# Memory values in four raw tiles of 256 columns, half of them worked off between the units of the memory attention

## The chip, the cores and the metric

One core of a Trainium2 chip runs the whole kernel. The metric is the device time of one execution in microseconds (us). The engines are TensorE (PE in the profile; its weight loads stand apart as PEld), VectorE (DVE), ScalarE (ACT), GpSimd (POOL) and SyncE (SP), whose queue issues the loads of the weights. The granted clock of TensorE has two levels, 2.4 GHz (1.00 in the rows) and 1.2 GHz (0.50).

## The reference

The kernel computes three transformer blocks in a row on 256 tokens of width 1024, in float32. The change lies in the first block, in and around its memory attention (4 heads of 256, 256 memory rows):

```python
def first_block(...):
    h = layer_norm(ALPHA * h + 0.5 * swiglu(h, ffn1_w1, ffn1_w3, ffn1_w2), ln1_g, ln1_b)
    mix = parallel_mixer(h, ...)                      # ends in (...) @ w_o
    h = layer_norm(ALPHA * h + mix, ln2_g, ln2_b)
    h = layer_norm(ALPHA * h + memory_attention(h, mem, mem_w_q, mem_w_kv, mem_w_o), ln3_g, ln3_b)
    ...

def memory_attention(h, mem, w_q, w_kv, w_o):
    q = (h @ w_q).reshape(B, S, 4, 256)
    k, v = split(mem @ w_kv)                          # each (B, M, 4, 256)
    s = einsum('bqhd,bkhd->bhqk', q, k) * 256 ** -0.5
    o = einsum('bhqk,bkhd->bqhd', softmax(s), v)
    return o.reshape(B, S, 1024) @ w_o
```

The keys and the values depend on `mem` alone, so they can be computed at any time before the attention needs them. The queries need the output of the second layer norm (`ln2`).

## The kernel before

**The weight stream.** All weights are packed on the host into slots of 128 x 1024 floats (512 KB). SP loads them in the order of the stages in `plan()` into a ring of 4 (`ring`); a slot's load waits until the slot four places earlier is free (`load`). There are two kinds of slots. A *split* slot is copied by ScalarE into a rounded high half (`wpair`, L477) and VectorE subtracts to get the low half (L480); its place in the ring is free after the subtraction, and TensorE later multiplies with three terms (high x high, high x low, low x high, in fp32r). There are three `wpair` buffers. A *raw* slot (the `False` in `plan()`: the memory keys and values among others) is read by TensorE straight from the ring in plain float32, which the trace shows as two instructions for each matmul; its place is free only when TensorE has gone on (`hold`, `release`).

**Stages.** `tok` stages (`pe_tok`) hold activations stationary and stream weights, in tiles of 512 columns; `feat` stages (`pe_feat`) hold weights stationary and stream 256 activations. A tile has two halves, t = 0 and 1: ScalarE takes the first out of PSUM and VectorE the second (`lin`). `lin_done0/1` count finished halves, `lin_out0/1` halves that were taken out, and `wait_lin(pe, g)` makes TensorE wait until g tiles have left. Every engine runs its list strictly in the order in which it is written.

**The order around the change**, on TensorE (L1694 to L1706): `memv0` (4 raw slots), with the transposes of `mix` after its 1st and 2nd slot; `wo` (8 split slots); `memv1` (4 raw slots), with the transposes of the normalised rows (`pe_norm`, in four quarters, each as soon as VectorE has written it) after its 2nd slot; `memq` (8 split slots, two tiles); `pe_attn(pe, MEM)`, four units of two heads and 128 queries each; the transposes of its output `mo`; `memo` (8 split slots); `pe_norm("ln3")`.

**The attention** is a pipeline: in step i TensorE computes the scores of unit i, the transposes of the probabilities of unit i-1 and the product with the values of unit i-2. VectorE takes the row maximum of the scores, ScalarE the exponentials and the copy of the transposed probabilities, and VectorE scales the result. `piece(i)` is a place behind the scores of unit i where other work can be put; the first block's other two attentions use it for the gate's weights (`pe_tok_piece`), the memory attention does not.

**Splitting ahead.** `split.begin(name, n)` makes ScalarE or VectorE split the first n slots of a stage at that place of its list; `split.cover(name, n)` splits up to two slots past tile n, but not past the next raw slot (`RUN_END`). Before `memv0` and `memv1` end, the lists read

```python
            act_x(act, "mix")            # and dve_x on VectorE
            split.begin("wo", 2)
            values_out(0)
            split.cover("wo")
            act_sqrt(act, "ln2")
            act_x(act, "ln2")
            split.begin("memq", 2)
            values_out(1)
            lin("memq", 0, ...)
            act_attn(act, MEM)
            act_x(act, "memo")
```

where `act_x` and `dve_x` (L722, L727) bring transposed rows as high and low half into `xpair`. As `memo` follows `memq` with no raw slot between, its first two slots are split while `memq` runs.

Of the kernel before, what the change touches and what calls it, by code (L numbers as in the profile page):

```python
# [30 lines left out]
P = 128  # L31
D = 1024
SEQ = 256
NT = SEQ // P
KD = D // P
# [39 lines left out]
def plan():  # L75

    stages = {}
    slot = tile = 0

    def add(name, kind, cols, ends, split, **more):  # L80
        nonlocal slot, tile
        stages[name] = Stage(kind, slot, tile, cols, ends, split, **more)
        slot, tile = slot + len(cols), tile + len(ends)

    def tok(name, nk, widths, split=True):
        s = Stage("tok", 0, 0, [], [], split, nk=nk)
        cols, ends = [], []
        for w in widths:
            kper = s.per_slot(w)
            cols += [min(kper, nk - k) * w for k in range(0, nk, kper)]  # L90
            ends.append(len(cols))
        add(name, "tok", cols, ends, split, widths=tuple(widths), nk=nk)

    def rows(name, nk, split=False):

        add(name, "rows", [SLOT] * nk, [nk, nk], split)

    def feat(name, ntile, split=True):
        add(name, "feat", [SLOT] * 4 * ntile, [4 * (n + 1) for n in range(ntile)], split)

    def ffn(name):
        add(name, "ffn", [SLOT] * 3 * NF, [3 * NF, 3 * NF], True)

    ffn("ffn0")
    feat("memk0", 1, False)
    tok("proj", KD, (384, 288, 512))
    feat("qkd", 2)
    tok("qb", Q_RANK // P, (384, 384), False)
    tok("kvb", KV_RANK // P, (512, 512), False)
    tok("gate", KD, (512,) * 4)  # L110
    feat("memk1", 1, False)
    tok("upm", 4, (512, 512))
    tok("upd", 4, (512, 512))
    tok("memv0", KD, (512,), False)
    tok("wo", KD, (512, 512))
    tok("memv1", KD, (512,), False)
    feat("memq", 2)
    tok("memo", KD, (512, 512))
    ffn("ffn1")
    for l in range(2):  # L120
        ffn(f"ffn{2 + 2 * l}")
        feat(f"cina{l}", 2)
        tok(f"bin{l}", KD, (512,))
        feat(f"cinb{l}", 2)
        rows(f"wout{l}", KD)
        ffn(f"ffn{3 + 2 * l}")
    tok("qkv", KD, (512,) * 6)
    tok("gatt", KD, (512, 512))
    tok("z", KD, (512,) * 4)
    tok("atto", KD, (512, 512), False)  # L130
    tok("dt", KD, (SSD_H,))
    feat("xbc", 8)
    tok("gssd", KD, (512, 512))
    rows("ssdo", INNER // P, True)
    tok("wo3", KD, (512, 512))
    feat("pq", 4)
    add("peer", "peer", [SLOT] * 2 * NKEY, [2 * NKEY] * 2, True)
    cols, order, run_end, count = [], [], [], [0, 0]
    for st in stages.values():
        for c in st.cols:  # L140
            cols.append(c)
            order.append((st.split, count[st.split]))
            count[st.split] += 1

    run_end = [0] * slot
    end = slot
    for i in reversed(range(slot)):
        if not order[i][0]:
            end = i
        run_end[i] = end  # L150
    return stages, slot, cols, order, run_end
# [64 lines left out]
def pack_stream(x):  # L216
# [3 lines left out]
    def put_tok(name, w):  # L220
        s = STAGES[name]
        slot, c0 = s.slot, 0
        for wd in s.widths:
            kper = s.per_slot(wd)
            blk = w[:, c0:c0 + wd].reshape(s.nk, P, wd)
            for k0 in range(0, s.nk, kper):
                kk = min(kper, s.nk - k0)
                out[slot, :, :kk * wd] = blk[k0:k0 + kk].transpose(1, 0, 2).reshape(P, kk * wd)
                slot += 1
            c0 += wd  # L230
# [27 lines left out]
    put_tok("wo", x["w_o"][0])  # L258
    for j in range(2):
        put_feat(f"memk{j}", x["mem_w_kv"][0][:, j * HALF:(j + 1) * HALF])  # L260
        put_tok(f"memv{j}", x["mem_w_kv"][0][:, D + j * HALF:D + (j + 1) * HALF])
    put_feat("memq", x["mem_w_q"][0])
    put_tok("memo", x["mem_w_o"][0])
    for l in range(2):
# [120 lines left out]
def build(nc, wstream, rows, mixrow, cols, diag, consts, relb, keys, x_tok, xT_in, memT_in, ws, out, tbuf):  # L385
    ctx = ExitStack()
    with ctx:
# [52 lines left out]
        def wait_lin(eng, g):  # L440

            if g > 0:
                for t in range(NT):
                    eng.wait_ge(S(f"lin_out{t}"), g)
# [74 lines left out]
        def bank(g, t):  # L519

            return psum[:, 2 * (g % 2) + t, :]
# [54 lines left out]
        FT0["peer"] = 6 * NF  # L576


        def pe_tok(pe, name, src, ns=range(8), between=lambda i: None):

            s = STAGES[name]
            slot = ([s.slot] + s.ends)[ns[0]]
            for n, w in enumerate(s.widths):
                if n not in ns:
                    continue
                g = s.tile + n
                kper = s.per_slot(w)
                if g >= 2:
                    wait_lin(pe, g - 1)
                for k0 in range(0, s.nk, kper):  # L590
                    ks = range(k0, min(k0 + kper, s.nk))
                    ws_ = weights(pe, slot)
                    for k in ks:
                        x_part(pe, k)
                    for t in range(NT):
                        for k in ks:
                            rhs = part(ws_, slice((k - k0) * w, (k - k0 + 1) * w))
                            end = k == s.nk - 1
                            products(pe, bank(g, t)[:, 0:w], src(k, t), rhs, k == 0, end,
                                     f"lin_done{t}" if end else None)  # L600
                    hold(slot)
                    slot += 1
                    between(slot - s.slot)

        def memk0_bank(g, t):
            return psum[:, 5 - t, :]
# [19 lines left out]
        def piece_bank(t):  # L626
            return psum[:, 2 + t, :]

        def pe_feat(pe, name, src, after=None, middle=None, between=lambda i: None, where=None):

            s = STAGES[name]
            for n in range(s.ntile):
                g = s.tile + n
                if g >= 2 and where is None:
                    wait_lin(pe, g - 1)
                for t in range(2):
                    for j in range(2):
                        slot = s.slot + 4 * n + 2 * t + j
                        w = weights(pe, slot)
                        for k in range(KD):  # L640
                            x_part(pe, k)
                            products(pe, (where or bank)(g, t)[:, j * SEQ:(j + 1) * SEQ],
                                     part(w, slice(k * P, (k + 1) * P)),
                                     [x_[:, k, :] for x_ in src], k == 0, k == KD - 1,
                                     f"lin_done{t}" if j == 1 and k == KD - 1 else None)
                        hold(slot)
                        between(slot + 1 - s.slot)
                    if t == 0 and middle is not None:
                        middle(n)
                if after is not None:  # L650
                    after(n)
# [595 lines left out]
        def ptbuf(i):  # L1247
            return region(PTB, 2, 2, SEQ)[:, i % 2]

        def pe_attn(pe, a, piece=lambda i: None):  # L1250
            n, u = a.units, a.u0
            for i in range(n + 2):
                if i < n:
                    if u + i >= 2:
                        pe.wait_ge(S("att_exp" if a.bias is None else "att_max"), u + i - 1)
# [359 lines left out]
        def _(pe):  # L1615
# [5 lines left out]
            def of(b, c0=0):  # L1621
                return lambda k, t: [b[:, c0 + k, tt(t)]]
# [71 lines left out]
            pe_tok(pe, "memv0", of(memT), between=mix_between)  # L1694
            x_comes("mix")
            pe_tok(pe, "wo", xt)
            pe_tok(pe, "memv1", of(memT), between=lambda i: pe_norm(pe, "ln2", res) if i == 2 else None)
            x_comes("ln2")
            pe_feat(pe, "memq", X)
            wait_lin(pe, STAGES["memo"].tile)  # L1700
            pe_attn(pe, MEM)
            pe.wait_ge(S("mo_ready"), 1)
            pe_transpose(pe, "memo", pairs(mo))
            x_comes("memo")
# [250 lines left out]
        def _(act):  # L1955
# [30 lines left out]
                                                     b if j else memk0_bank(0, 0)))  # L1986

            def values_out(j):
                lin(f"memv{j}", 0, lambda n, b: copy(mvv[:, 0, j * HALF:(j + 1) * HALF], b))

            keys_out(0)
            lin("proj", 0, lambda n, b: copy([cq[:, 0, :], ckv[:, 0, :], vd[:, 0].rearrange("p h d -> p (h d)")][n],
# [56 lines left out]
            act_x(act, "ln2")  # L2049
            split.begin("memq", 2)  # L2050
            values_out(1)
            lin("memq", 0, lambda n, b: copy(mqT[:, 4 * n:4 * n + 2, :].rearrange("p c s -> p (c s)"), b))
            act_attn(act, MEM)
            act_x(act, "memo")
            split.cover("memo", more=1)
            act_sqrt(act, "ln3")
# [219 lines left out]
        def _(dve):  # L2276
# [34 lines left out]
                                                     b if j else memk0_bank(0, 1)))  # L2311

            def values_out(j):
                lin(f"memv{j}", 1, lambda n, b: copy(mvv[:, 1, j * HALF:(j + 1) * HALF], b))

            keys_out(0)
            lin("proj", 1, lambda n, b: copy([cq[:, 1, :], ckv[:, 1, :], vd[:, 1].rearrange("p h d -> p (h d)")][n],
# [143 lines left out]
            for name in ("upm", "upd"):  # L2461
# [23 lines left out]
            dve_x(dve, "ln2")  # L2485
            split.begin("memq", 2)
            values_out(1)
            lin("memq", 1, lambda n, b: copy(mqT[:, 4 * n + 2:4 * n + 4, :].rearrange("p c s -> p (c s)"), b))
            dve_attn(dve, chain, MEM, lambda j, o: scaled(
                j, o, mo[:, j % 2, 512 * (j // 2):512 * (j // 2) + 512].rearrange("p (e d) -> p e d", e=2), 256))  # L2490
            dve.nop().then_inc(S("mo_ready"), 1)
            dve_x(dve, "memo")
            split.cover("memo", more=1)
            rows = Rows(dve, chain, "memo", 1.0 / ALPHA)
# [593 lines left out]
```

## Time and profile before

| | us |
|---|---|
| median of 3 runs | 3134.42 |
| lowest and highest run | 3133.32, 3137.1 |
| the profiled execution, its own time | 3132.71 |
| its span in the trace | 3130.9 |
| TensorE busy in the span | 3000.7 (96%) |
| VectorE, ScalarE busy | 2012.7 (64%), 1356.3 (43%) |
| mean granted clock | 0.982 |

The span is what the trace covers; the execution's own time is 1.8 us longer. Busy times of TensorE are those of pipelined instructions, so neighbouring rows overlap by a few tenths of a us. The stage of the change lies between 412 and 545 us.

### The profile page before, as it was taken

The page shows a single profiled execution, that of the slowest core. Times are in us where ns is not written, and L with a number is a line of the kernel's source. Part 1 is how long each engine was busy: PE and PEld are TensorE (multiplying, and loading weights), DVE is VectorE, ACT ScalarE, POOL GpSimd, SP SyncE. Part 2 cuts the span into 40 slices and gives each one's busy share as a digit, 9 for nine tenths or more (in the row PEclk, how much of TensorE's full clock was granted, in tenths as well). Part 3 has the DMA queues.
Part 4 walks back from the last instruction along what each step waited for, and adds up shares of the span by engine and source line. Part 5 has one row for each costly group of instructions (what it writes and reads, how often), then busy time and mean ns, then how long its engine had stood idle before and what let it go on. Part 6 is the DMA issues. An engine that isn't in the chain of part 4 may idle for free.

```text
span 3130.9 us, 52632 instructions
## 1 busy us (share of the span) xinstructions
PE 3000.7 (96%) x19072; PEld 2668.6 (85%) x19072; DVE 2012.7 (64%) x3581; ACT 1356.3 (43%) x1983; POOL 182.6 (6%) x196
## 2 busy tenths in 40 slices
PE   8999998998999999999999999998898899999998
PEld 8987767997989798998799776987797888888887
DVE  5565665556557556556755663897599866776665
ACT  4333434434443344435244553654446744434333
POOL 0000000000000000000000000000057700000000
PEclk9999999999999999999999999999999999999999
DMA  7564353555554555555455643523442255555554
GB/s 273 187 216 149 106 183 128 188 187 201 186 177 142 211 185 177 192 187 174 147 185 186 197 140 124 172 88 115 141 158 91 71 185 188 190 182 181 176 183 143
DMA packets 140271, 523.73 MB, mean 167 GB/s; under 512 B 15650, under 2 KB 15650, under 8 KB 137312
## 3 DMA queue, kind: packets, MB, share of 16 engines
q1 hardware_dynamic: 134768, 490.79, 47.1%
q0 software_dynamic: 4784, 29.94, 2.5%
q8 instruction: 95, 1.56, 0.2%
q10 hardware_dynamic: 576, 1.05, 0.1%
q14 instruction: 48, 0.39, 0.0%
HBM read 520.65 MB, written 1.06 MB: 167 GB/s over the span
## 4 chain that ended last, share of the span: by engine, by line
PE 75%; DVE 10%; ACT 3%; issue 2%; DMA 0%; ACTq 0%; DVEq 0%; SPq 0%
PE psum L509 68%; PE psum L1759 2%; DVE wpair L480 1%; PE psum L1943 1%; ACT wpair L477 1%; PE psum L664 1%; PE psum L1744 1%; ACT arena L1304 0%; DVE small L3027 0%; DVE arena L3006 0%; PE psum L1287 0%; PE psum L1207 0%; DVE st L1334 0%; PE psum L1263 0%; DVE arena L2917 0%
## 5 line engine op out<-in xcount | busy, mean ns | idle before, releaser
L480 DVE TENSOR_TENSOR wpair<-ring,wpair 128x1024 fp32r<-128x1024 f32 (+1 forms) x862 | 1044.5, 1220 | 744.1 <-ACT wpair L477 740.1
L509 PE MATMUL psum<-xpair,wpair 128*128 128x256 f32 x11712 | 1477.3, 285 | 19.1 <-DVE wpair L480 12.6
L509 PEld LDWEIGHTS psum<-xpair,wpair 128*128 128x128 f32 x11712 | 1446.2, 193 | 56.5 <-DVE wpair L480 32.6
L477 ACT CAST wpair<-ring 128x1024 fp32r<-128x1024 f32 (+1 forms) x888 | 919.0, 1044 | 817.0 <-PE psum L509 737.3
L509 PE MATMUL psum<-wpair,hpair 128*128 128x512 f32 x3120 | 753.5, 392 | 7.7 <-DVE hpair L939 7.7
L509 PEld LDWEIGHTS psum<-wpair,hpair 128*128 128x128 f32 x3120 | 573.7, 189 | 121.0 <-issue 10.7
L509 PE MATMUL psum<-wpair,xpair 128*128 128x512 f32 (+3 forms) x1728 | 401.7, 391 | 5.0 <-DVE wpair L480 1.8
L509 PEld LDWEIGHTS psum<-wpair,xpair 128*128 128x128 f32 x1728 | 320.8, 192 | 74.3 <-issue 6.8
L914 ACT ACTIVATE small<-psum 128x256 f32<-128x256 f32 x132 | 50.7, 384 | 232.7 <-PE psum L509 232.7
L950 ACT ACTIVATE small<-psum 128x256 f32<-128x256 f32 x92 | 35.4, 384 | 262.1 <-PE psum L509 262.1
L928 DVE TENSOR_TENSOR small<-small,psum 128x256 f32<-128x256 f32 x132 | 55.6, 421 | 137.8 <-ACT small L914 137.8
L939 DVE TENSOR_TENSOR hpair<-small,hpair 128x256 fp32r<-128x256 f32 x236 | 100.4, 425 | 8.1
L1565 POOL DMA_DIRECT2D arena<-rows x18 | 9.6, 532 | 1533.4 <-DVEq L1122 1186.7
L1943 PE MATMUL psum<-hpair,small 128*128 128x128 f32 x512 | 70.5, 281 | 12.3 <-ACT hpair L2255 10.2
L1943 PEld LDWEIGHTS psum<-hpair,small 128*128 128x128 f32 x512 | 63.2, 193 | 17.2 <-DVE small L3027 14.7
L3027 DVE TENSOR_SCALAR small<-kc,small 128x128 f32<-128x128 f32 x256 | 76.8, 342 | 0.1
L937 DVE CAST hpair<-small 128x256 fp32r<-128x256 f32 x236 | 69.4, 294 | 8.1
L480 POOL TENSOR_TENSOR wpair<-ring,wpair 128x1024 fp32r<-128x1024 f32 x26 | 62.5, 2408 | 164.3 <-DVE wpair L480 148.5
L722 ACT CAST xpair<-psum 128x512 fp32r<-128x512 f32 x60 | 34.2, 587 | 66.5 <-PE psum L664 39.7
L1000 DVE TENSOR_TENSOR small<-small,arena 128x256 f32<-128x256 f32 x92 | 60.9, 662 | 0.0
L1304 ACT ACTIVATE arena<-arena,st 128x128 f32<-128x128 f32 (+1 forms) x64 | 28.6, 447 | 72.5 <-DVE st L1334 72.5
L1225 DVE SCALAR_TENSOR_TENSOR arena<-arena,pcol 128x256 f32<-128x256 f32 x144 | 58.9, 480 | 1.1 <-DVE arena L2616 0.5
(330 smaller groups left out, 1845.5 us busy)
## 6 DMA issues: line engine op xcount, KB each, us to landing
ring<-wstream SPq DMA_DIRECT2D x934, 512.0 KB, 3.3
arena<-rows POOLq DMA_DIRECT2D x18, 1024.0 KB, 5.2
arena<-diag POOLq DMA_DIRECT2D x2, 1728.0 KB, 10.5
arena<-tbuf POOLq DMA_DIRECT2D x2, 1024.0 KB, 9.0
arena<-x_feat ACTq DMA_DIRECT2D x4, 256.0 KB, 7.5
res<-x_tok POOLq DMA_DIRECT2D x1, 1024.0 KB, 6.7
gb<-mem_feat POOLq DMA_DIRECT2D x1, 1024.0 KB, 15.1
arena<-keys POOLq DMA_DIRECT2D x1, 1024.0 KB, 7.2
```

The lines of the kernel that those rows point to most:

```text
L477: eng.copy(hi, raw).then_inc(S("w_hi"), 1)
L480: eng.tensor_tensor(wpair[:, 1, o % PAIRS, 0:w], raw, hi.bitcast(F32), ALU.subtract)\
L509: mm = pe.matmul(out_, a[i], b[j], start=start and n == 0, stop=stop_ and last)
L914: act.activation(gated(f0 + f), psum[:, 4 + (f0 + f) % 2, 0:SEQ], ACT.Silu).then_inc(S("hid_act"), 1)
L928: dve.tensor_tensor(whole(h), gated(h), psum[:, 4 + h % 2, SEQ:2 * SEQ], ALU.mult)\
L937: dve.tensor_copy(hpair[:, 0, h % 2, :], src).then_inc(S("hid_hi"), 1)
L939: dve.tensor_tensor(hpair[:, 1, h % 2, :], src, hpair[:, 0, h % 2, :].bitcast(F32), ALU.subtract)\
L1000: dve.tensor_tensor(whole(h), gated(f), weight(f + step * i), ALU.mult).then_inc(S("hid_whole"), 1)
L1225: chain.mark(eng.scalar_tensor_tensor(out=acc[:, f, :], in0=src, scalar=w, in1=acc[:, f, :], op0=ALU.mult, op1=ALU.add))
L1759: mm = pe.matmul(bank(st_out.tile + n, t), catT[:, WOUT_K[j], tt(t)], ws_[j][:, n * HALF:(n + 1) * HALF], start=(j == 0), stop=(j == KD - 1))
L1943: mm = pe.matmul(psum[:, n % 4, j * P:(j + 1) * P], oh1[:, n % 2, j, :], oh2[:, n % 2, j, :].bitcast(F32), start=True, stop=True)
L3027: ins = dve.tensor_scalar(oh1[:, n % 2, j, :], iota, selT[:, 0, tok], selT[:, 2, tok], ALU.is_equal, ALU.mult)
```

## The change

The memory values become four raw tiles of 256 columns (2 slots each, the same 8 slots in all). `memv0` and `memv1` keep their places, with two slots instead of four; the transposes of `ln2` move from behind the second to behind the first slot of `memv1`. `memv2` and `memv3` stand behind `memq` in the stream and are computed in the pieces behind the scores of units 2 and 3, into PSUM banks 2 and 3. The second tile of `memq` is computed in the pieces behind units 0 and 1, two slots each (`pe_feat_slot`). TensorE gets waits before units 0, 2 and 3 and before step 4 for the tiles that they need, and ScalarE and VectorE take the tiles out in the middle of their attention steps (`mem_amid`). As the stream now has raw slots between `memq` and `memo`, the first two slots of `memo` are split by a `begin` of their own behind the attention.

```diff
-    tok("memv0", KD, (512,), False)
+    tok("memv0", KD, (256,), False)
     tok("wo", KD, (512, 512))
-    tok("memv1", KD, (512,), False)
+    tok("memv1", KD, (256,), False)
     feat("memq", 2)
+    tok("memv2", KD, (256,), False)
+    tok("memv3", KD, (256,), False)
     tok("memo", KD, (512, 512))
...
+        def late_values(j):
+            return lambda t: psum[:, 2 + t, (j - 2) * SEQ:(j - 1) * SEQ]
...
+        def pe_feat_slot(pe, name, i, src):
+
+            s = STAGES[name]
+            w = weights(pe, s.slot + i)
+            t, j = i % 4 // 2, i % 2
+            for k in range(KD):
+                products(pe, piece_bank(t)[:, j * SEQ:(j + 1) * SEQ], part(w, slice(k * P, (k + 1) * P)),
+                         [x_[:, k, :] for x_ in src], k == 0, k == KD - 1,
+                         f"lin_done{t}" if j == 1 and k == KD - 1 else None)
+            hold(s.slot + i)
...
-            pe_tok(pe, "memv1", of(memT), between=lambda i: pe_norm(pe, "ln2", res) if i == 2 else None)
+            pe_tok(pe, "memv1", of(memT), between=lambda i: pe_norm(pe, "ln2", res) if i == 1 else None)
             x_comes("ln2")
-            pe_feat(pe, "memq", X)
-            wait_lin(pe, STAGES["memo"].tile)
-            pe_attn(pe, MEM)
+            pe_feat(pe, "memq", X, ns=(0,))
+            sq = STAGES["memq"]
+
+            def mem_before(i):
+                if i in (0, 2):
+                    wait_lin(pe, sq.tile + 1 + i // 2)
+                if i == 3:
+                    wait_lin(pe, STAGES["memv3"].tile)
+                if i == 4:
+                    wait_lin(pe, STAGES["memo"].tile)
+
+            def mem_piece(i):
+                if i < 2:
+                    for j in range(2):
+                        pe_feat_slot(pe, "memq", 4 + 2 * i + j, X)
+                else:
+                    pe_tok(pe, f"memv{i}", of(memT), where=late_values(i))
+
+            pe_attn(pe, MEM, mem_piece, mem_before)
...
             split.begin("memq", 2)
             values_out(1)
-            lin("memq", 0, lambda n, b: copy(mqT[:, 4 * n:4 * n + 2, :].rearrange("p c s -> p (c s)"), b))
-            act_attn(act, MEM)
+            def queries_out(n):
+                lin("memq", 0, lambda n, b: copy(mqT[:, 4 * n:4 * n + 2, :].rearrange("p c s -> p (c s)"),
+                                                 b if n == 0 else piece_bank(0)), (n,))
+
+            def mem_amid(i):
+                if i == 0:
+                    split.cover("memq", 1)
+                if i == 1:
+                    queries_out(1)
+                if i in (2, 3):
+                    values_out(i)
+
+            queries_out(0)
+            act_attn(act, MEM, mem_amid)
+            split.begin("memo", 2)
             act_x(act, "memo")
```

VectorE's list changes in the same way (its `split.begin("memo", 2)` stands behind the signal `mo_ready` and ahead of `dve_x`).

## Rows read from the trace of the kernel before

**Rows 1.** Page: busy time of TensorE; the chain that ended last, by engine.

```profile
PE 3000.7 (96%) x19072; PEld 2668.6 (85%) x19072; DVE 2012.7 (64%) x3581; ACT 1356.3 (43%) x1983; POOL 182.6 (6%) x196
...
PE 75%; DVE 10%; ACT 3%; issue 2%; DMA 0%; ACTq 0%; DVEq 0%; SPq 0%
```

**Rows 2.** Timeline of TensorE from 405 to 545: start, length, line, count [idle before].

```profile
412.70 3.60 PE L509 MATMUL psum<-ring,gb 128*128 128x512 f32 x8
416.14 1.04 PE L664 MATMUL psum<-kc,arena 128*128 128x128 f32 x8
...
420.45 1.04 PE L664 MATMUL psum<-kc,arena 128*128 128x128 f32 x8
...
427.79 22.37 PE L509 MATMUL psum<-wpair,xpair 128*128 128x512 f32 x96
449.99 7.03 PE L509 MATMUL psum<-ring,gb 128*128 128x512 f32 x16
...
459.19 0.66 PE L1207 MATMUL psum<-kc,res 128*128 128x128 f32 x4 [0.79 <-DVE res L1114]
459.69 7.03 PE L509 MATMUL psum<-ring,gb 128*128 128x512 f32 x16
466.16 23.59 PE L509 MATMUL psum<-xpair,wpair 128*128 128x256 f32 x192
490.58 3.69 PE L1263 MATMUL psum<-gb,arena 128*128 128x256 f32 x16 [0.83 <-issue]
494.59 0.66 PE L1276 MATMUL psum<-kc,arena 128*128 128x128 f32 x4 [0.32 <-ACT arena L1304]
...
503.45 3.70 PE L1287 MATMUL psum<-arena 128*128 128x256 f32 x16
508.26 1.09 PE L664 MATMUL psum<-kc,arena 128*128 128x128 f32 x8 [1.11 <-DVEq L2491]
510.32 1.25 PE L664 MATMUL psum<-kc,arena 128*128 128x128 f32 x8 [0.96 <-DVE xpair L727]
511.33 22.05 PE L509 MATMUL psum<-wpair,xpair 128*128 128x512 f32 x96
```

**Rows 3.** Busy time by stage, the memory attention: us, PE, PEld, DVE, ACT, POOL, clock, DMA.

```profile
487.00:508.00 21.00, 19.01 (x103) 16.05 (x102) 8.64 (x18) 8.90 (x23) 0.00 (x0) 1.00 0.16 52
```

**Rows 4.** Timeline of TensorE in `memk1`: raw slots with 256 columns streamed.

```profile
383.10 3.62 PE L509 MATMUL psum<-gb,ring 128*128 128x256 f32 x16
386.55 1.04 PE L664 MATMUL psum<-kc,arena 128*128 128x128 f32 x8
```

**Rows 5.** Timeline of VectorE from 415 to 545.

```profile
423.13 1.23 DVE L480 TENSOR_TENSOR wpair<-ring,wpair 128x1024 fp32r<-128x1024 f32 x1
...
453.84 0.75 DVE L1114 SCALAR_TENSOR_TENSOR res<-res,st,arena 128x512 f32<-128x512 f32 x1
...
461.69 2.35 DVE L480 TENSOR_TENSOR wpair<-ring,wpair 128x1024 fp32r<-128x1024 f32 x2
...
509.57 1.29 DVE L727 TENSOR_TENSOR xpair<-psum,xpair 128x512 fp32r<-128x512 f32 x2 [1.42 <-ACT xpair L722]
```

**Rows 6.** Timeline of TensorE: work behind gaps elsewhere in the kernel.

```profile
360.46 0.66 PE L1276 MATMUL psum<-kc,arena 128*128 128x128 f32 x4 [3.00 <-ACT arena L1304]
...
937.74 1.32 PE L1207 MATMUL psum<-kc,arena 128*128 128x128 f32 x8 [1.64 <-DVE arena L1106]
...
1048.33 1.32 PE L1207 MATMUL psum<-kc,arena 128*128 128x128 f32 x8 [1.64 <-DVE arena L1106]
```

**Rows 7.** Busy time by stage behind those gaps: granted clock is third from the end.

```profile
362.00:364.00 2.00, 2.00 (x10) 1.90 (x10) 1.01 (x6) 1.97 (x2) 0.00 (x0) 0.55 0.03 8
364.00:366.00 2.00, 2.00 (x6) 1.53 (x6) 1.93 (x6) 1.91 (x1) 0.00 (x0) 0.60 0.00 0
...
940.00:945.00 5.00, 4.36 (x21) 3.99 (x20) 4.40 (x8) 3.06 (x4) 0.53 (x1) 0.50 0.29 102
1045.00:1050.00 5.00, 3.15 (x13) 1.37 (x12) 3.90 (x8) 4.03 (x12) 0.00 (x0) 1.00 0.06 9
```

More of the change, by code:

```diff
@@ L260, in pack_stream @@
         put_feat(f"memk{j}", x["mem_w_kv"][0][:, j * HALF:(j + 1) * HALF])
-        put_tok(f"memv{j}", x["mem_w_kv"][0][:, D + j * HALF:D + (j + 1) * HALF])
+    for j in range(4):
+        put_tok(f"memv{j}", x["mem_w_kv"][0][:, D + j * SEQ:D + (j + 1) * SEQ])
     put_feat("memq", x["mem_w_q"][0])
@@ L576, in build, with pe_tok @@
         FT0["peer"] = 6 * NF
-        def pe_tok(pe, name, src, ns=range(8), between=lambda i: None):
+        def pe_tok(pe, name, src, ns=range(8), between=lambda i: None, where=None):
             s = STAGES[name]
@@ L589, in pe_tok @@
                     wait_lin(pe, g - 1)
+                dst = where or (lambda t: bank(g, t)[:, 0:w])
                 for k0 in range(0, s.nk, kper):
@@ L598, in pe_tok @@
                             end = k == s.nk - 1
-                            products(pe, bank(g, t)[:, 0:w], src(k, t), rhs, k == 0, end,
+                            products(pe, dst(t), src(k, t), rhs, k == 0, end,
                                      f"lin_done{t}" if end else None)
@@ L627, in piece_bank, with pe_feat @@
             return psum[:, 2 + t, :]
-        def pe_feat(pe, name, src, after=None, middle=None, between=lambda i: None, where=None):
+        def pe_feat_slot(pe, name, i, src):
[7 more added lines that the diff above has]
+            hold(s.slot + i)
+        def pe_feat(pe, name, src, after=None, middle=None, between=lambda i: None, where=None, ns=range(8)):
             s = STAGES[name]
             for n in range(s.ntile):
+                if n not in ns:
+                    continue
                 g = s.tile + n
@@ L1248, in ptbuf, with pe_attn @@
             return region(PTB, 2, 2, SEQ)[:, i % 2]
-        def pe_attn(pe, a, piece=lambda i: None):
+        def pe_attn(pe, a, piece=lambda i: None, before=lambda i: None):
             n, u = a.units, a.u0
             for i in range(n + 2):
+                before(i)
                 if i < n:
@@ L1988, in values_out @@
             def values_out(j):
-                lin(f"memv{j}", 0, lambda n, b: copy(mvv[:, 0, j * HALF:(j + 1) * HALF], b))
+                lin(f"memv{j}", 0, lambda n, b: copy(mvv[:, 0, j * SEQ:(j + 1) * SEQ],
+                                                     b[:, 0:SEQ] if j < 2 else late_values(j)(0)))
             keys_out(0)
@@ L2313, in values_out @@
             def values_out(j):
-                lin(f"memv{j}", 1, lambda n, b: copy(mvv[:, 1, j * HALF:(j + 1) * HALF], b))
+                lin(f"memv{j}", 1, lambda n, b: copy(mvv[:, 1, j * SEQ:(j + 1) * SEQ],
+                                                     b[:, 0:SEQ] if j < 2 else late_values(j)(1)))
             keys_out(0)
@@ L2487, in _, with queries_out, mem_amid @@
             values_out(1)
-            lin("memq", 1, lambda n, b: copy(mqT[:, 4 * n + 2:4 * n + 4, :].rearrange("p c s -> p (c s)"), b))
+            def queries_out(n):
+                lin("memq", 1, lambda n, b: copy(mqT[:, 4 * n + 2:4 * n + 4, :].rearrange("p c s -> p (c s)"),
+                                                 b if n == 0 else piece_bank(1)), (n,))
+            def mem_amid(i):
+                if i == 0:
+                    split.cover("memq", 1)
+                if i == 1:
+                    queries_out(1)
+                if i in (2, 3):
+                    values_out(i)
+            queries_out(0)
             dve_attn(dve, chain, MEM, lambda j, o: scaled(
-                j, o, mo[:, j % 2, 512 * (j // 2):512 * (j // 2) + 512].rearrange("p (e d) -> p e d", e=2), 256))
+                j, o, mo[:, j % 2, 512 * (j // 2):512 * (j // 2) + 512].rearrange("p (e d) -> p e d", e=2), 256),
+                mem_amid)
             dve.nop().then_inc(S("mo_ready"), 1)
+            split.begin("memo", 2)
             dve_x(dve, "memo")
```

## Prediction, made before the changed kernel ran

> **What bounds the kernel now.** I read the page first: TensorE is busy 96% of the span and carries 75% of the chain that ended last [rows 1], so the question is only where TensorE idles around the change. The timeline of TensorE over the stage answers that [rows 2]. From the start of `memv0` (412.70) to the start of `memo` (511.33), 98.6 us, its gaps are 0.79 (the last quarter of `ln2`), 0.83 (the queries leave PSUM before the first scores), 0.32 (the first exponentials), 1.11 and 0.96 (around the transposes of `mo`): 4.0 us in all. The memory attention, 490.58 to 507.15, holds only the gap of 0.32.
>
> Is that attention really full? Matmul rows are pipelined, so busy time alone does not show it. The rate does: 16 instructions of 256 float32 columns take 3.69 us in the scores and 3.70 in the value products [rows 2], and 16 of the same shape take 3.62 in a raw slot of the keys, where nothing waits [rows 4]. The attention runs at the rate of a plain stream. What is put between its units is therefore paid in full, and the change can only win what it takes off elsewhere.
>
> **The change part by part.** *Slot price.* A raw slot of 512-column values takes 416.14 - 412.70 = 3.44 us with 8 instructions [rows 2]. With 256 columns it has 16; the keys' slot of that shape takes 386.55 - 383.10 = 3.45 [rows 4]. Equal, so smaller tiles cost nothing, and the eight slots stay 27.5 us. Four of them (two of `memv0`, two of `memv1`) move into the attention, four split slots of `memq` too.
>
> *A, ahead of `wo`: two slots of 3.44 leave.* They cover the way from the transposed `mix` to the first split weights. TensorE now ends the second transposes at 420.45 + 1.04 = 421.49 [rows 2]. VectorE's list goes on with the low half of x and then, behind ScalarE's cast, the low half of the first `wo` slot, which ends at 423.13 + 1.23 = 424.36 [rows 5]. `wo` needs it, and the two slots that hid this now start behind it. So `wo` starts at about 424.4 instead of 427.79: 3.4 us won, not 6.9, and a new gap of 2.9.
>
> *B, around `ln2`: one slot leaves ahead of the transposes and one behind.* Count from the end of `wo` (449.99 now). VectorE writes the first quarter at +4.60 (453.84 + 0.75) [rows 5]; the fourth's transposes start as soon as VectorE has written it, at 459.19, +9.20, and the next work follows at 459.69 [rows 2]. That is VectorE's time, whatever TensorE did before. The slot removed ahead wins nothing: TensorE waits four times, 4.60 + 0.05 - 3.44 = 1.2 us, then about 1.0 three times (quarters come (9.20 - 4.65) / 3 = 1.5 apart, their transposes take 0.5), 4.2 us instead of 0.79. Behind them one slot remains. `memq` could then start 3.0 to 3.4 us later, but its first low half ends at 461.69 + 1.23 = 462.92 [rows 5], so it starts at 463.0 instead of 466.16: 3.2 won. A and B together win 6.6.
>
> *C, in the attention: four raw slots come, 4 x 3.44 = 13.8.* The moved `memq` slots keep their length: two tiles took 23.59 [rows 2], of which four slots now run between units. Added waits: `wait_lin` before unit 0 is the old gap of 0.83. The one before unit 2 is a second gap of that kind, since the second query tile leaves PSUM right before its scores; the 0.44 of unit 0's transposes covers part, so 0.4 to 0.8; I take 0.8. Queued behind it on TensorE are unit 2's scores and all that follows. In exchange the 0.32 goes, as pieces cover the exponentials. The waits before unit 3 and step 4 stand behind transposes and a value product of 1.7 us, while the copy of 512 columns or less needs under 0.83: nothing, unless ScalarE or VectorE is late (below). Each step from raw to split slots starts some 0.2 to 0.4 early, which the rows show as overlap: -0.4. C without its end: 13.8 + 0.5 - 0.4 = 13.9.
>
> *D, the start of `memo`.* Its first two slots were split under `memq`. Now VectorE subtracts them between `mo_ready` and the low half of x: 2.35 as a pair (the length of the pair in [rows 5]). Today that low half starts 1.31 behind the first transposes (509.57 against 508.26) [rows 2, 5]; it will start about 2.3 behind, as VectorE begins the pair about when TensorE begins the transposes: +0.95. TensorE's third transpose group queues behind it, and then `memo`. Bounds 0 and 2.35.
>
> *Loads.* Four raw slots now stand on SP's queue between `memq` and `memo`. Each takes the place of a `memq` slot that is freed by its split, more than 10 us before its piece. `memo`'s fourth slot waits for the last raw place, freed with the first transposes of `mo`; TensorE needs it some 12 us later. Nothing. The ring turns freer ahead of `wo`, but `wo` is bound by TensorE: nothing.
>
> *Sum:* -6.6 + 13.9 + 0.95 = 8.3 us.
>
> *The clock.* The new gaps have a price of their own. Behind a gap of 3.00 us at 360.46 [rows 6] the granted clock was 0.55 and 0.60 over four us [rows 7], half speed for part of it, which loses 2 x 0.45 + 2 x 0.40 = 1.7 us of work. A gap of 1.64 ahead of norm transposes was followed by 0.50 over five us in one place and by 1.00 in another [rows 6, 7]. [...] From the rows: A's 2.9 is nearest to the 3.00, so 1.7. B idles 4.2 of 6.2 us, more than the 1.64 pattern: 0 to 3.4, and I take one fall, 1.7. D lies between its old gaps (no fall, 1.00) and a fall: 0 to 1.7, I take 0. That gives 8.3 + 3.4 = 11.7.
>
> **Rivals.** *1. The attention has hidden room (within 0.2%).* Weight loads are busy 16.05 of 21 us in the attention [rows 3]. If the unloaded share, 24%, were room, 16.6 x 0.24 = 4.0 us of the streamed work would be free and the sum 8.3 - 4.0 = 4.3, with the clock held: 3137. The Trainium skill ("Perfetto Trace Analysis", its opening note) holds weight-load busy time for a better measure than matmul busy time; the equal rates above speak against reading room from it here. The same end comes if A or B idles less and no clock falls: +4 to +6. Chance 0.15.
>
> *2. The other side: faster.* If scores and value products were bound by the softmax's latencies and not by TensorE, the pieces would fill them. The four raw slots would have to vanish but for 6.6 us of their 13.8, so 7.2 of 16.6 us would have to be hidden idle, and 8.3 with C's wait and D paid; from there on the kernel gets faster. With all of the 13.8 hidden the kernel ends at 3132.7 - 6.6 + 0.5 + 0.95 - 0.4 = 3127. For it: transposes between units do wait for ScalarE. Against it: one gap of 0.32 and the rate. Chance 0.06.
>
> *3. Slower yet.* ScalarE and VectorE take tiles out in the middle of a step, in order. A copy that waits for a piece holds back the copy of the probabilities or the next maximum, and TensorE then waits in each unit. Price: up to 0.83 in each of three later steps, and both extra falls of the clock (1.7 for B, 1.7 for D): 3144.4 + 2.5 + 3.4 = 3150. Against it: the half that ScalarE takes is finished half a slot earlier, and 1.7 us of value products follow each piece. Chance 0.09.
>
> **How the numbers follow.** My case, 8 to 14 us more, has 0.70. The sum is made against the profiled execution's own time: 3132.7 + 11.7 = 3144.4; its own range is 3140.5 (no fall) to 3148. The median of the runs stands 1.7 above that execution, so the median should come out between 3144.4 and 3146.1: 3145. Later norm stages fall in clock or not by chance (the 1.64 pattern did both), so any shift in time may add or take a fall or two of 1.7: +-3. The range takes half of rival 1 and most of rival 3: 3136 to 3151. 0.2% is 6.3 us, about what a measurement can tell from no change. Slower by more: 0.70 + 0.09 = 0.79; within: 0.15; faster: 0.06.
>
> **What would show it.** In the trace after: a gap near 2.9 ahead of `wo`, `wo` starting near 424.4; four gaps of about 1 us around the `ln2` transposes; `memq` starting near 459.7 (6.5 earlier); pieces of 5.9 and 6.9 us between units with no shorter attention work beside them; the transposes of `mo` near 515.6 and `memo` near 519.7, both later by the clock's loss; and a granted clock below 1.00 shortly behind the first gap. Wrong would be: scores and products shorter than before once pieces lie between them, raw slots other than 3.44, or no gap in A.

## The result and the profile after

| | before | after |
|---|---|---|
| median of 5 runs, us | 3136.19 | 3149.86 |
| lowest and highest run, us | 3133.32, 3137.1 | 3142.89, 3154.19 |
| the profiled execution, its own time, us | 3132.71 | 3142.89 |
| from the start of `memv0` to the start of `memo`, us | 98.63 | 111.09 |

The changed kernel takes 1.0042 times the time of the one before, 95% interval 1.0032 to 1.0053: slower by 13 us, forecast 3145 in 3136 to 3151. The stage is 12.46 us longer. The profiled executions differ by only 10.2, because the stretch ahead of the stage, which the change does not touch, was 2.7 us shorter (`memv0` starts at 410.00 instead of 412.70); behind the start of `memo` both spans have 2619.6 us left. The profile after is that of the fastest of the five runs.

The timeline of TensorE after, over the same stage as [rows 2] (start, length, line, count, idle before):

```profile
410.00 3.61 PE L512 MATMUL psum<-ring,gb 128*128 128x256 f32 x16
...
417.79 1.04 PE L684 MATMUL psum<-kc,arena 128*128 128x128 f32 x8
421.95 23.66 PE L512 MATMUL psum<-wpair,xpair 128*128 128x512 f32 x96 [3.13 <-DVE wpair L483]
445.46 3.62 PE L512 MATMUL psum<-ring,gb 128*128 128x256 f32 x16
450.11 0.66 PE L1227 MATMUL psum<-kc,res 128*128 128x128 f32 x4 [1.04 <-DVE res L1134]
451.56 0.66 PE L1227 MATMUL psum<-kc,res 128*128 128x128 f32 x4 [0.79 <-DVE res L1134]
453.20 0.66 PE L1227 MATMUL psum<-kc,res 128*128 128x128 f32 x4 [0.99 <-DVE res L1134]
454.65 1.11 PE L1227 MATMUL psum<-kc,res 128*128 128x128 f32 x4 [0.79 <-DVE res L1134]
455.56 6.18 PE L512 MATMUL psum<-ring,gb 128*128 128x256 f32 x16
461.39 11.86 PE L512 MATMUL psum<-xpair,wpair 128*128 128x256 f32 x96
474.08 1.97 PE L1284 MATMUL psum<-gb,arena 128*128 128x256 f32 x8 [0.83 <-issue]
475.69 6.11 PE L512 MATMUL psum<-xpair,wpair 128*128 128x256 f32 x48
481.64 1.89 PE L1284 MATMUL psum<-gb,arena 128*128 128x256 f32 x8
...
490.19 1.97 PE L1284 MATMUL psum<-arena 128*128 128x256 f32 x8 [0.46 <-issue]
491.99 7.07 PE L512 MATMUL psum<-ring,gb 128*128 128x256 f32 x32
498.90 0.60 PE L1297 MATMUL psum<-kc,arena 128*128 128x128 f32 x4
...
517.03 1.09 PE L684 MATMUL psum<-kc,arena 128*128 128x128 f32 x8 [1.11 <-DVEq L2556]
520.08 1.25 PE L684 MATMUL psum<-kc,arena 128*128 128x128 f32 x8 [1.96 <-DVE xpair L747]
521.09 22.05 PE L512 MATMUL psum<-wpair,xpair 128*128 128x512 f32 x96
```

The single gap of 0.79 around `ln2` [rows 2] has become four, a gap of 3.13 stands ahead of `wo`, the pieces between the units take 5.9 to 6.9 us each and nothing in the attention got shorter for them. Two rows are longer than their work: `wo` at 23.51 to the next row instead of 22.20, and the last value slot at 5.83 instead of 3.45. Busy time by stage shows why (granted clock third from the end):

```profile
421.00:425.00 4.00, 3.05 (x10) 2.47 (x11) 3.30 (x4) 1.60 (x3) 0.00 (x0) 0.77 0.56 148
425.00:430.00 5.00, 5.00 (x20) 4.02 (x19) 1.23 (x1) 1.43 (x2) 0.00 (x0) 0.84 0.55 196
...
453.00:457.00 4.00, 3.00 (x12) 2.50 (x13) 3.82 (x7) 1.78 (x3) 0.53 (x1) 0.61 0.28 65
457.00:460.00 3.00, 3.00 (x9) 2.37 (x8) 2.59 (x3) 2.06 (x4) 0.00 (x0) 0.50 0.69 287
460.00:464.00 4.00, 4.00 (x28) 3.72 (x27) 1.56 (x2) 0.54 (x1) 0.00 (x0) 0.91 0.22 76
```

The clock fell twice, behind the gap ahead of `wo` and within the gaps around `ln2`. Summed as in the prediction, the first two rows lost 4 x 0.23 + 5 x 0.16 = 1.7 us of TensorE's work, the other three 4 x 0.39 + 3 x 0.50 + 4 x 0.09 = 3.4. Before, none of this stage ran below 1.00:

```profile
423.00:441.00 18.00, 18.00 (x70) 12.87 (x69) 8.37 (x8) 6.98 (x8) 0.00 (x0) 1.00 0.64 220
...
457.00:487.00 30.00, 29.21 (x204) 25.05 (x202) 16.82 (x18) 12.44 (x15) 0.53 (x1) 1.00 0.64 229
```

### The profile page after: what moved, and what is told of

The parts are those of the page before. It is cut to its first block, busy times and chain, and to the rows that moved or that the text cites. A ratio compares the mean times of both kernels' runs of the same rounds, so it can differ in the third digit from the quotient of the medians.

```text
span 3140.7 us, 52771 instructions
## 1 busy us (share of the span) xinstructions
PE 3003.8 (96%) x19136; PEld 2683.9 (85%) x19136; DVE 2012.0 (64%) x3583; ACT 1356.3 (43%) x1985; POOL 182.7 (6%) x196
## 4 chain that ended last, share of the span: by engine, by line
PE 83%; DVE 11%; ACT 3%; issue 2%; DMA 1%; ACTq 0%; DVEq 0%; SPq 0%
PE psum L512 76%; PE psum L1796 2%; DVE wpair L483 1%; PE psum L1980 1%; ACT wpair L480 1%; PE psum L684 1%; DMA ring<-wstream 1%; PE psum L1781 1%; DVE small L3093 0%; PE psum L1284 0%; PE psum L1308 0%; DVE arena L3072 0%; ACT arena L1325 0%; DVE st L1355 0%; PE psum L1227 0%
## 5 line engine op out<-in xcount | busy, mean ns | idle before, releaser
L1980 PE MATMUL psum<-hpair,small 128*128 128x128 f32 x512 | 71.3, 283 | 12.3 <-ACT hpair L2306 10.2
## 6 DMA issues: line engine op xcount, KB each, us to landing
arena<-diag POOLq DMA_DIRECT2D x2, 1728.0 KB, 10.2
```

What stands on the lines that cost most here:

```text
L1980: mm = pe.matmul(psum[:, n % 4, j * P:(j + 1) * P], oh1[:, n % 2, j, :], oh2[:, n % 2, j, :].bitcast(F32), start=True, stop=True)
```

## The experiments

Times of the stage (`memv0` to `memo`) come from each kernel's profile; ratios are against the kernel before on the same chip. The theory is that of the prediction: the attention has no room, and the value slots that were taken away had covered waits, which cost a second time in the clock.

**1. Work in the new gaps.** The changed kernel, with multiplies that need nothing and whose results nobody reads.

```diff
+        def filler(pe, n, b):
+            for _ in range(n):
+                release(pe.matmul(psum[:, b, 0:SEQ], ident, memT[:, 0, :], start=True, stop=True))
...
+                    filler(pe, 7, 4)            # behind the second transposes of mix
...
+                filler(pe, fill[i], quarter_bank(name, i))   # ln2: fill = (2, 1, 2, 1)
                 pe.wait_ge(S("normed"), 4 * NORMS.index(name) + i + 1)
```

> The changed kernel with extra float32 multiplies of 256 columns (results never read) where TensorE now waits: 7 ahead of wo, and 2, 1, 2, 1 ahead of the four quarters of ln2. From the start of memv0 to the start of memo the changed kernel took 111.1 us, the one before 98.6. Theory (beside the uncovered waits, 4.5 us are lost to the clock that falls behind them: wo at 23.5 us instead of 22.2, and the last value slots and transposes of ln2 some 3.2 us longer): with TensorE kept at work wo takes 22.2 again, the granted clock stays at 1.00 from 420 to 465, and the stage takes 106.6. Rival (the long wo and the long value slots have another cause, as loads or reads that collide): the stage stays at 111 or grows by the work that was added.

Measured: ratio 1.0028 (1.0016 to 1.0040), stage 519.30 - 412.75 = 106.55 us. Its timeline of TensorE:

```profile
421.40 3.19 PE L1219 MATMUL psum<-gb,kc 128*128 128x256 f32 x14
424.70 22.01 PE L512 MATMUL psum<-wpair,xpair 128*128 128x512 f32 x96
446.55 3.61 PE L512 MATMUL psum<-ring,gb 128*128 128x256 f32 x16
...
456.24 3.62 PE L512 MATMUL psum<-ring,gb 128*128 128x256 f32 x16
459.71 11.75 PE L512 MATMUL psum<-xpair,wpair 128*128 128x256 f32 x96
...
518.29 1.32 PE L684 MATMUL psum<-kc,arena 128*128 128x128 f32 x8 [1.96 <-DVE xpair L747]
519.30 23.65 PE L512 MATMUL psum<-wpair,xpair 128*128 128x512 f32 x96
```

and its busy time by stage:

```profile
421.00:425.00 4.00, 3.89 (x21) 3.18 (x19) 3.07 (x4) 3.83 (x6) 0.00 (x0) 1.00 0.35 131
...
457.00:460.00 3.00, 3.00 (x16) 2.49 (x15) 3.00 (x5) 3.00 (x5) 0.00 (x0) 1.00 0.89 347
```

`wo` starts 11.95 us behind `memv0`, exactly as without the added work, and takes 21.85; the last value slot takes 3.47 again; the granted clock is 1.00 from 405 to 516. So 4.5 of the 12.5 us were the clock's. The loss has not wholly gone: here the clock fell behind the gap of 1.96 at the end (`memo` takes 23.65), where it had held in the changed kernel's own profile. The gap is the same; whether the clock falls behind it is not. In the time of the whole kernel this version is not told apart from the change (1.0042, 1.0032 to 1.0053); it is the stage that shows the clock's share.

**2. Is there room in the attention?** The kernel before with 32 such instructions between the units.

```diff
-            pe_attn(pe, MEM)
+            pe_attn(pe, MEM, lambda i: filler(pe, 8, i) if i in (2, 3) else None)
```

> The kernel before with 16 extra instructions (8 float32 multiplies of 256 columns, nothing loaded, results never read) behind the scores of unit 2 of the memory attention and 16 behind those of unit 3. Theory (the attention has no room): all 32 are paid at 0.216 each, the stage from memv0 to memo goes from 98.6 to 105.5 us. Rival (a quarter of the attention is room, as its weight-load row suggests): about 4 us vanish, 101.5. Rival (the attention is bound by the softmax's latencies): 98.6 to 99.

Measured: ratio 1.0026 (1.0017 to 1.0036), stage 517.19 - 411.90 = 105.29 us, 6.66 more; the instructions themselves take 3.45 to 3.46 a piece of sixteen:

```profile
495.99 3.62 PE L1199 MATMUL psum<-gb,kc 128*128 128x256 f32 x16
499.45 0.60 PE L1280 MATMUL psum<-kc,arena 128*128 128x128 f32 x4
...
503.34 3.62 PE L1199 MATMUL psum<-gb,kc 128*128 128x256 f32 x16
506.79 0.60 PE L1280 MATMUL psum<-kc,arena 128*128 128x128 f32 x4
```

All but 0.25 us was paid: no room. Rivals 1 (by its 24% of unloaded time) and 2 fall. The Trainium skill ("Perfetto Trace Analysis", its opening note) sends the reader to the weight-load busy time; here 76% of it [rows 3] stood over a stretch without room, and the spacing of equal instructions was the measure that held.

**3. Smaller tiles alone.** Four tiles of 256 columns in the old places.

```diff
-    tok("memv0", KD, (512,), False)
+    tok("memv0", KD, (256,), False)
+    tok("memv1", KD, (256,), False)
     tok("wo", KD, (512, 512))
-    tok("memv1", KD, (512,), False)
+    tok("memv2", KD, (256,), False)
+    tok("memv3", KD, (256,), False)
```

> The kernel before with its values in four tiles of 256 columns, all in the old places (two tiles ahead of wo, two around ln2). Theory (a slot costs the same in either shape): stage 98.6 us within 0.5, time the same within 0.2%. Rival (twice as many instructions, more copies): up to 8 slots x 0.1 to 0.2 us more, 99.5 to 100.

Measured: stage 510.62 - 411.88 = 98.74 us, as before: in this stage the shape costs nothing. The ratio is 1.0012 (1.0003 to 1.0021), some 4 us that this stage does not hold. In the profiles 3.3 us lie behind the start of `memo` (3133.5 - 510.62 = 2622.9 against 2619.6); summed over slices of 4 us, the granted clock lost 53.2 us of TensorE's work there, before 49.7. A little more lies outside the span: these runs outlast it by 1.9 to 3.0 us, those of the kernel before by 1.8. Whether the shape has to do with either stays open.

**4. The queries alone.** The second query tile between the units, values untouched.

```diff
+                if i < 2:
+                    for j in range(2):
+                        pe_feat_slot(pe, "memq", 4 + 2 * i + j, X)
```

> One part alone: the second tile of the memory queries is computed behind the scores of units 0 and 1, the values stay in two tiles of 512 in their old places, and the first slots of memo are split early as before. Theory: nothing is uncovered and nothing is gained, one more wait of 0.46 us before unit 2 against the 0.32 and some overlap: stage 98.0 to 99.0 us. Rival (streaming fills the attention): below 97. Rival (copies in the middle of a step hold up ScalarE and VectorE): above 100.

Measured: ratio 1.0004 (0.9994 to 1.0014), stage 512.02 - 411.54 = 100.48 us, above what I expected. TensorE, then ScalarE:

```profile
495.11 1.99 PE L1281 MATMUL psum<-arena 128*128 128x256 f32 x8 [1.59 <-ACT arena L2081]
...
510.45 1.91 PE L681 MATMUL psum<-kc,arena 128*128 128x128 f32 x8 [0.96 <-DVE xpair L744]
512.02 22.95 PE L509 MATMUL psum<-wpair,xpair 128*128 128x512 f32 x96
```

```profile
486.12 1.04 ACT L477 CAST wpair<-ring 128x1024 fp32r<-128x1024 f32 x1 [2.15 <-PE psum L1281]
490.41 1.05 ACT L477 CAST wpair<-ring 128x1024 fp32r<-128x1024 f32 x1 [3.25 <-PE psum L509]
493.56 0.47 ACT L1322 ACTIVATE arena<-psum,st 128x256 f32<-128x256 f32 x1 [2.10 <-DVE st L1348]
...
494.47 0.58 ACT L2081 COPY arena<-psum 128x512 f32<-128x512 f32 x1
```

That is rival 3's mechanism, in a kernel where it could show. With no raw slot between `memq` and `memo`, `cover` in the middle of step 0 also splits `memo`'s first slots, whose `wpair` buffers come free only in piece 1. Both engines stand there (VectorE's subtraction at 491.49 waits 3.07 us for ScalarE's cast, and unit 1's maximum follows only at 492.63); unit 1's exponentials start at 493.56, the query copy follows, and TensorE waits 1.59. With the old 0.32 gone and a fall of the clock at the end (1.57 from the last transposes to `memo` instead of the 1.01 of [rows 2]) that is 1.59 - 0.32 + 0.56 = 1.83 of the 1.85 us. In the changed kernel the raw slots stop `cover`, and the wait is 0.46. What the `begin` behind the attention costs (0.99, below) is thus the price of not having this.

**5 and 6. Each place alone.** One tile streamed behind unit 3's scores, taken from ahead of `wo` (order `memv0`, `wo`, `memv1`, `memv2`, `memq`, `memv3`) or from around `ln2` (`memv0`, `memv1`, `wo`, `memv2`, `memq`, `memv3`). In both `memo`'s first slots are split behind the attention, as in the change.

```diff
-            pe_attn(pe, MEM)
+            pe_attn(pe, MEM, lambda i: pe_tok(pe, "memv3", of(memT), where=late_values) if i == 3 else None,
+                    lambda i: wait_lin(pe, STAGES["memo"].tile) if i == 4 else None)
```

> Only the slots ahead of wo are moved: two of the eight value slots (one tile of 256) leave that place and are computed behind the scores of unit 3; around ln2 four slots stay, the whole of memq runs ahead of the attention, memo's first slots are split behind the attention. Stage from memv0 to memo, 98.6 us before, 111.1 with the whole change. Theory, from the terms as they were measured: 3.1 us won ahead of wo, 1.3 lost again where the clock falls behind the gap, 6.9 paid in the attention, 0.95 at memo: 104.7 (103.4 if the clock holds), and around ln2 the old single gap of 0.79. Rival (the place ahead of wo hid nothing, all 6.9 are won there): 99.6.

> Only the slots around ln2 are moved: four value slots stay ahead of wo, two around ln2 with its transposes behind the first, two behind the scores of unit 3, memq ahead of the attention, memo's first slots split behind the attention. Theory: 3.2 us won, up to 3.4 lost to the clock, 6.9 paid, 0.95 at memo: 103.3 us with the clock held, 106.5 with a fall; four gaps of 0.8 to 1.0 us around the transposes and none ahead of wo. Rival (slots around ln2 hid nothing): 99.6.

Measured: ahead of `wo` ratio 1.0017 (1.0007 to 1.0026), stage 515.58 - 411.10 = 104.48 us; around `ln2` 1.0015 (1.0005 to 1.0025), stage 519.41 - 414.05 = 105.36 us. The timeline of the first, then of the second:

```profile
423.06 23.65 PE L512 MATMUL psum<-wpair,xpair 128*128 128x512 f32 x96 [3.13 <-DVE wpair L483]
446.54 7.07 PE L512 MATMUL psum<-ring,gb 128*128 128x256 f32 x32
...
455.75 0.66 PE L1213 MATMUL psum<-kc,res 128*128 128x128 f32 x4 [0.79 <-DVE res L1120]
```

```profile
456.08 0.66 PE L1213 MATMUL psum<-kc,res 128*128 128x128 f32 x4 [1.04 <-DVE res L1120]
457.53 0.66 PE L1213 MATMUL psum<-kc,res 128*128 128x128 f32 x4 [0.80 <-DVE res L1120]
459.18 1.12 PE L1213 MATMUL psum<-kc,res 128*128 128x128 f32 x4 [0.99 <-DVE res L1120]
460.63 1.11 PE L1213 MATMUL psum<-kc,res 128*128 128x128 f32 x4 [0.33 <-DVE res L1120]
461.53 5.61 PE L512 MATMUL psum<-ring,gb 128*128 128x256 f32 x16
```

Each place shows its own gaps and its own fall of the clock, and each tile is paid in the attention; both stages are near what was expected and far from the rivals' 99.6. Together they make 5.85 + 6.73 = 12.6 with the end's 0.99 counted twice; the whole change made 12.46 with one end and one wait more. Both places hid something; neither was spare.

**7. `memo`'s first slots earlier.** The changed kernel with `split.begin("memo", 2)` behind step 3 on ScalarE and in step 4 on VectorE.

```diff
-            act_attn(act, MEM, mem_amid)
-            split.begin("memo", 2)
+            act_attn(act, MEM, mem_amid, lambda i: split.begin("memo", 2) if i == 3 else None)
```

> The changed kernel with the first two slots of memo split inside the last steps of the attention (ScalarE behind unit 2's probabilities, VectorE ahead of unit 2's result). Theory: the low half of x follows the first transposes of mo at 1.31 us again, the gap of 1.96 between them goes back to 0.96, the stage goes from 111.1 to 110.2 where the clock does as before. Rival (the splits hold up the last unit's copy): the value products of units 2 and 3 no longer follow each other and the stage stays at 111 or grows.

Measured: ratio 1.0035 (1.0024 to 1.0045), stage 519.93 - 411.38 = 108.55 us. From the first transposes of `mo` to `memo` it takes 519.93 - 516.87 = 3.06 instead of 4.06, the second gap is 0.96 again. One microsecond is the split's; the other 1.5 us of the stage are a shorter fall of the clock around `ln2` (the last value slot takes 4.17 instead of 5.83), which this edit does not touch. In the time of the whole kernel the difference to the change (1.0042, 1.0032 to 1.0053) can't be told.

**8. The old gaps closed, nothing streamed.** The kernel before, two waits moved.

```diff
-            pe_tok(pe, "memv1", of(memT), between=lambda i: pe_norm(pe, "ln2", res) if i == 2 else None)
+            pe_tok(pe, "memv1", of(memT), between=lambda i: pe_norm(pe, "ln2", res) if i == 3 else None)
...
-            wait_lin(pe, STAGES["memo"].tile)
-            pe_attn(pe, MEM)
+            wait_lin(pe, STAGES["memo"].tile - 1)
+            pe_attn(pe, MEM, before=lambda i: wait_lin(pe, STAGES["memo"].tile) if i == 2 else None)
```

> The kernel before, with nothing streamed: the transposes of ln2 stand behind the third slot of memv1 instead of the second, and unit 0 waits only for the first tile of queries, unit 2 for the second. Theory: the gaps of 0.79 and 0.83 close, the stage goes from 98.6 to 97.0 us; the time falls by 0.05%, too little to be told. Rival (one slot behind the transposes is too little cover, memq waits for its first low half): memq starts as late as before or later, 97.8 or more.

Measured: ratio 0.9992 (0.9982 to 1.0001), stage 513.09 - 415.69 = 97.40 us. The gaps of 0.79 and 0.83 are gone; a new one of 0.17 ahead of `memq` is the rival's, small (`memq` starts 15.80 us behind the end of `wo` instead of 16.17). Of the 0.4 us above the 97.0 expected, 0.5 are a fall of the clock at the end: from the last transposes to `memo` it takes 513.09 - 511.56 = 1.53 instead of 1.01, behind a gap of 0.97 that passed at 0.96 before. No difference in time can be told.

**9 and 10. Work in the gaps of the norms.** Experiment 1 points beyond the change: the kernel before has gaps like these at most norms. The kernel before with fillers there, alone and with the edit of 8. Three each stand ahead of six norms (the expectation says seven).

```diff
+        FILLS = {"ln2": (0, 0, 0, 0), "ln1": (0, 0, 0, 0), "ln3": (10, 2, 2, 2), "n1_0": (23, 0, 0, 0),
+                 "norm1": (11, 0, 0, 0)}
...
+            fill = FILLS.get(name, (3, 0, 0, 0))
```

> The kernel before, its streaming untouched, with extra float32 multiplies of 256 columns (results never read) where TensorE waits for the norms: 10, 2, 2, 2 ahead of the quarters of ln3, 23 ahead of n1_0, 11 ahead of norm1, 3 ahead of each of the seven norms that wait 1.64 us. Theory (TensorE pays for its gaps twice, the second time at half clock): no stretch at 0.50 behind these norms any more; about 1.5 us won at ln3, 2 each at n1_0 and norm1, 2.3 at each of the others where the clock fell (three of seven in the profile of before): 8 to 13 us, a ratio of 0.996 to 0.9975. Rival (the clock behind the norms costs nothing, as VectorE sets the pace there): same time. Rival (the added work is in the way): slower.

> The same extra multiplies at the norms, with the transposes of ln2 behind the third slot of memv1 and unit 0 waiting only for the first tile of queries. Theory: the sum of both, 9 to 14 us less than before. Rival: as for the norms alone.

Measured: alone 3122.98 us against 3135.53, ratio 0.9959 (0.9945 to 0.9972), 12.6 us faster, within the 8 to 13 expected; with 8, 3127.14 us, ratio 0.9965 (0.9952 to 0.9979), no different from the first within the intervals, so that the edit of 8 adds nothing that can be told. The first quarter of `ln3` before:

```profile
537.91 1.11 PE L1207 MATMUL psum<-kc,res 128*128 128x128 f32 x4 [4.53 <-DVE res L1114]
```

`ln3` in the timeline of the first:

```profile
534.71 4.48 PE L1199 MATMUL psum<-gb,kc 128*128 128x256 f32 x20
539.40 0.66 PE L1216 MATMUL psum<-kc,res 128*128 128x128 f32 x4 [0.21 <-DVE res L1114]
...
545.57 11.98 PE L509 MATMUL psum<-xpair,wpair 128*128 128x256 f32 x96 [0.97 <-DVE xpair L727]
```

and its busy time by stage at the norm at 937 of [rows 6, 7]:

```profile
940.00:945.00 5.00, 4.17 (x34) 3.79 (x32) 4.86 (x8) 3.07 (x5) 0.53 (x1) 1.00 0.50 170
```

The clock reads 1.00 where it read 0.50, and the mean over the execution rises from 0.982 to 0.990. At `ln3` the gain stands behind the gap and not in it: the next multiplies start 545.57 - 512.82 = 32.75 us behind `memo`, before 544.09 - 511.33 = 32.76, and their 96 take 11.82 us to the next row instead of 12.88. By the mean clock (an estimate) (1 - 0.982) x 3130.9 = 56 us were lost to the clock before and (1 - 0.990) x 3121.5 = 31 now; of these 25 us about half came back as time. The rest was lost where TensorE waited anyway: before, it was busy for 1.36 of the 5 us from 740 to 745, at 0.50. This version beats both kernels, and it has nothing of the change in it.

## Why the prediction was right

Term by term, forecast against the timeline after:

| term | forecast, us | measured, us |
|---|---|---|
| A, start of `wo` behind `memv0` | -3.4 | 11.95 - 15.09 = -3.14 |
| the clock behind A | +1.7 | 23.51 - 22.20 = +1.31 |
| B, end of `wo` to `memq`, with its clock | -3.2 + 1.7 = -1.5 | 15.93 - 16.17 = -0.24 |
| C, `memq` to the transposes of `mo` | +13.9 | 55.64 - 42.10 = +13.54 |
| D, from there to `memo` | +0.95 | 4.06 - 3.07 = +0.99 |
| sum | +11.65 | +12.46 |

The main step, that the attention is full and its guests pay, is shown by experiment 2. That the removed slots were cover is shown by 5 and 6: the gap of 2.9 came out at 3.13, the four of 1.0 to 1.2 at 1.04, 0.79, 0.99 and 0.79. D is shown by 7. Without the clock the sum was forecast at 8.3; with the clock held in A and B (experiment 1) it is 106.55 - 98.63 = 7.9.

The term that was mis-sized is the clock around `ln2`. I took one fall, 1.7 us; experiment 1 needs 13.16 us from the end of `wo` to `memq` where the changed kernel took 15.93, so it cost 2.8, within the bounds of 0 to 3.4. In experiment 7 the same gaps cost 1.7 less at the last value slot. The rows of the result say the same: 3.4 us of work lost around `ln2`, twice what I took, of which 2.8 were paid. Without the clock B won 16.17 - 13.16 = 3.0 us where I had 3.2. The second error is small: A's gap is 0.25 longer since TensorE starts that much behind the end of the subtraction. The 1.7 for A was the right size: the rows lost 1.7, and against experiment 1 `wo` took 23.51 - 21.85 = 1.66 longer.

The sum is shown for the profiled execution; that the median fell into the range is in part luck. The profiled execution came 1.5 us below its forecast (3142.89 for 3144.4) though the stage came 0.8 above: the stretch ahead of the stage was 2.7 us shorter, where the clock lost 3.4 us instead of 5.1, summed over slices of 4 us. From it to the median I allowed 1.7 us, and it was 7.0, so that the median stands 4.9 above the forecast and 1.1 below the end of the range. The median moved by 13.7 us, the stage by 12.5. The rest is not traced: the five runs of the changed kernel lie between 3142.89 and 3154.19, and falls of the clock that come or stay away (at `memo` in experiment 1, around `ln2` in 7) are of this size. A part lies outside the span: the runs of the changed kernel outlast theirs by 2.2 to 3.2 us, those of the kernel before by 1.8 in each of its 67 runs beside the experiments, and no run shows why.

The Trainium skill ("TensorE: Matmul & The Clock Gate", section "HAM oscillation — how this bites in real kernels") describes a kernel that waited for data between bursts of matmuls, long enough to lose the clock at each wait. That such a loss is paid, experiment 1 agrees: `wo` took 23.51 us behind the gap of 3.13 and 21.85 with the gap filled. It is no rule for the shorter gaps here: the gap of 1.96 at the end passed at 1.00 in the profile after, and the clock fell behind it in experiment 1.

## What to carry to other kernels

Before moving work into a stage, compare the spacing of its instructions with the same instructions in a stretch that waits for nothing: if they are equal, as here (3.69 and 3.62 us for sixteen), expect the stage to be full, however many handovers it has. Independent work next to a chain of small steps is cover; count the chain without it before taking it away, and add the clock behind the new gap. Where nothing useful is left for such a gap, multiplies that nobody reads can be worth more than the idle time.

## What was not expected of the hardware

The 68 extra multiplies of about 0.43 us each, placed only where TensorE waited, made the whole kernel 12.6 us faster, nearly as much as the change cost. And like gaps do not always have like consequences: the same gap of 1.96 us ahead of `memo` was followed by 22.05 us for its 96 multiplies in one profile and 23.65 in another; a gap of 0.96 there was followed by 22.05 before and by 22.95 in experiment 4.
